# One accumulator per tile: the three products of a split fp32r block as 256-column matmuls into the same PSUM columns

## The reference, cut to what matters

```python
h = rmsnorm(x, g_pre_mix[l])
proj = h @ w_in[l]
q_in, ckv, k_rope, lru_x, lru_y, gate_mla, gate_lru = jnp.split(proj, IN_SPLIT_IDX, axis=-1)
o_mla = mla_attention(q_in, ckv, k_rope, positions, g_ckv[l], w_ukv[l]) @ w_o_mla[l]
...
merged = jax.nn.sigmoid(gate_mla) * o_mla + jax.nn.sigmoid(gate_lru) * o_lru
x = x + rmsnorm(merged @ w_out[l], g_post_mix[l])
...
x = x + rmsnorm(co @ w_co[l], g_post_x[l])
h = rmsnorm(x, g_pre_ffn[l])
up = causal_dwconv(h @ w_up[l], w_fconv[l], b_fconv[l])
gate, val = jnp.split(up, 2, axis=-1)
x = x + rmsnorm((jax.nn.gelu(gate, approximate=True) * val) @ w_down[l], g_post_ffn[l])
```

## Time and profile before

| | |
|---|---|
| median of 3 runs | 1879.62 us (1879.6 to 1880.23) |
| span of the profiled execution | 1877.5 us |
| the runs' median beside that span | 2.1 us more, for what lies around it |
| PE busy | 1798.7 us, 96% of the span |
| DVE, ACT, POOL busy | 1215.4, 973.1, 334.2 us |
| mean granted TensorE clock | 0.981 of full speed |

### The profile page before, as it was taken

How to read it: one execution, slowest core, us unless ns; L and a number is a source line. 1 busy time by engine, 2 the same in 40 slices (tenths; PEclk the granted TensorE clock), 3 DMA queues, 4 the chain that set the end, 5 groups by cost and what they waited for, 6 DMA issues and landing times.

```text
span 1877.5 us, 29213 instructions
## 1 busy us (share of the span) xinstructions
PE 1798.7 (96%) x10026; PEld 1547.0 (82%) x10026; DVE 1215.4 (65%) x1508; ACT 973.1 (52%) x1265; POOL 334.2 (18%) x375
## 2 busy tenths in 40 slices
PE   6999999999999999999998779999999999999995
PEld 5788888888888888888887558888888888888884
DVE  5666665455688874447465568776457776567776
ACT  5555555453577664445345545555345554345552
POOL 0001110000244431112243360010000000000074
PEclk9999999999999999999999879999999999999997
DMA  6544445656555565666645225657645667656561
GB/s 216 185 134 135 134 157 175 206 174 195 157 190 183 179 197 189 195 192 209 198 147 168 91 68 179 200 179 185 196 157 187 194 185 199 195 171 194 162 169 45
DMA packets 344230, 322.50 MB, mean 172 GB/s; under 512 B 5792, under 2 KB 334196, under 8 KB 343412
## 3 DMA queue, kind: packets, MB, share of 16 engines
q1 hardware_dynamic: 339124, 314.51, 53.7%
q10 hardware_dynamic: 5056, 7.34, 1.1%
HBM read 319.73 MB, written 2.10 MB: 171 GB/s over the span
## 4 chain that ended last, share of the span: by engine, by line
PE 86%; DVE 6%; ACT 3%; issue 2%; POOL 2%; DMA 0%; ACTq 0%; DVEq 0%; POOLq 0%
PE ps L414 80%; ACT wsp L822 2%; DVE wsp L1176 2%; POOL scr L1724 2%; PE ps L430 1%; PE ps L571 1%; PE ps L570 1%; PE ps L619 1%; DVE hsp L1472 1%; PE ps L477 1%; DVE big_b L1466 1%; DVE big_b L1618 0%; DVE scr L1197 0%; DMA big_a<-in_x 0%; PE ps L584 0%
## 5 line engine op out<-in xcount | busy, mean ns | idle before, releaser
L414 PE MATMUL ps<-hsp,wsp 128*128 128x512 f32 (+1 forms) x6432 | 1157.2, 341 | 19.7 <-DVE wsp L1176 8.6
L414 PEld LDWEIGHTS ps<-hsp,wsp 128*128 128x128 f32 x6432 | 992.1, 189 | 175.0 <-issue 14.0
L1176 DVE TENSOR_TENSOR wsp<-raw,wsp 128x2048 fp32r<-128x2048 f32 (+2 forms) x312 | 707.7, 2287 | 232.9 <-ACT wsp L822 230.1
L822 ACT ACTIVATE wsp<-raw 128x2048 fp32r<-128x2048 f32 (+2 forms) x312 | 580.5, 1884 | 13.8 <-PE ps L414 10.2
L414 PE MATMUL ps<-asp,wsp 128*128 128x512 f32 (+1 forms) x2816 | 505.5, 341 | 9.0 <-DVE scr L1295 4.4
L414 PEld LDWEIGHTS ps<-asp,wsp 128*128 128x128 f32 x2816 | 435.8, 190 | 75.9 <-DVE scr L1295 4.7
L833 ACT ACTIVATE cr<-ps 128x256 f32<-128x256 f32 x337 | 126.7, 381 | 546.2 <-PE ps L414 525.0
L1758 POOL TENSOR_TENSOR scr<-scr 128x256 f32<-128x256 f32 x44 | 34.2, 797 | 630.0 <-DVE scr L1556 630.0
L1184 DVE TENSOR_TENSOR cr<-ps,cr 128x256 f32<-128x256 f32 x140 | 56.9, 420 | 105.3 <-ACT cr L833 104.6
L1110 ACT ACTIVATE scr<-scr,par 128x256 f32<-128x256 f32 x88 | 48.2, 595 | 63.3 <-DVE scr L1545 63.3
L1678 POOL TENSOR_TENSOR scr<-scr 128x256 f32<-128x256 f32 x16 | 28.6, 1787 | 256.7 <-ACT scr L968 256.7
(11 more groups left out here) (180 smaller groups left out, 944.8 us busy)
## 6 DMA issues: line engine op xcount, KB each, us to landing
raw<-in_w_up SPq DMA_DIRECT2D x88, 1024.0 KB, 5.2
raw<-in_w_in SPq DMA_DIRECT2D x64, 1024.0 KB, 5.3
raw<-in_w_down SPq DMA_DIRECT2D x32, 1024.0 KB, 6.1
raw<-in_w_in SPq DMA_DIRECT2D x32, 768.0 KB, 4.2
raw<-in_w_o_mla SPq DMA_DIRECT2D x16, 1024.0 KB, 6.0
raw<-in_w_o_lru SPq DMA_DIRECT2D x16, 1024.0 KB, 5.6
raw<-in_w_out SPq DMA_DIRECT2D x16, 1024.0 KB, 5.5
raw<-in_w_down SPq DMA_DIRECT2D x16, 768.0 KB, 5.1
```

What stands on the lines that cost most here:

```text
L414: mm = pe.matmul(ps[:, bank, 0:w], lhs(part, k), x[:, 0:w], start=(f and part == 0), stop=(l and n == 1))
L822: act.activation(wsp[:, p0 % SLOTS, 0, 0:n], raw[:, p0 % SLOTS, 0:n], ACT.Copy).then_inc(hi_done, 1)
L1176: dve.tensor_tensor(wsp[:, slot, 1, 0:n], raw[:, slot, 0:n], wsp[:, slot, 0, 0:n].bitcast(F32), ALU.subtract).then_inc(lo_done, 1)
```

## The change

Each k now takes three matmuls of 256 columns, all into the first 256 columns of the bank, in the order high-high, high-low, low-high. `cross`, the buffer `cr` and the semaphores `cross_done` and `gate_done` are gone; DVE copies a finished tile from PSUM (`take`), and where a second operation followed the sum it now reads PSUM itself. The sigmoid of GM on ACT reads PSUM as well. In the first round of UP the tiles are taken out by `unit`, which stands behind `rms(7)`.

```diff
+TERMS = [(0, 0), (0, 1), (1, 0)]
...
                     f, l = first and k == 0, last and k == kn - 1
-                    parts = [1, 0] if l and not f else [0, 1]
-                    for n, part in enumerate(parts):
-                        w = T if part else 2 * T
-                        mm = pe.matmul(ps[:, bank, 0:w], lhs(part, k), x[:, 0:w], start=(f and part == 0),
-                                       stop=(l and n == 1))
+                    for n, (part, low) in enumerate(TERMS):
+                        mm = pe.matmul(ps[:, bank, 0:T], lhs(part, k), x[:, low * T:(low + 1) * T],
+                                       start=(f and n == 0), stop=(l and n == 2))
...
-            def cross(ph, i, j, slot=None, bank=None, scaled=None):
...
-                act.activation(cr[:, slot, :], ps[:, bank, T:2 * T], ACT.Copy).then_inc(cross_done, 1)
...
-            def add(ph, i, j, dst, slot=None, bank=None):
...
-                dve.wait_ge(cross_done, ph.t(i, j) + 1)
-                return dve.tensor_tensor(dst, ps[:, bank, 0:T], cr[:, slot, :], ALU.add)
+            def tile_done(ph, i, j):
+
+                dve.wait_ge(gemm_step, ph.g(i, ph.done[j]))
+
+            def take(ph, i, j, dst, bank=None):
+
+                tile_done(ph, i, j)
+                return dve.tensor_copy(dst, ps[:, j % 4 if bank is None else bank, 0:T])
...
-                    def sums(v):
-                        for j in (2 * v, 2 * v + 1):
-                            add(up, i, j, cr[:, j, :]).then_inc(tile_out, 1)
-
                     def unit(v):
 
                         for e in range(2):
-                            dve.wait_ge(tile_out, up.t(i, 2 * v + e) + 1)
-                            dve.tensor_tensor(UR[2 * v + e], cr[:, 2 * v + e, :], RR, ALU.mult).then_inc(up_ready, 1)
+                            tile_done(up, i, 2 * v + e)
+                            dve.tensor_tensor(UR[2 * v + e], ps[:, 2 * v + e, 0:T], RR, ALU.mult).then_inc(tile_out, 1)
...
                     if first:
-                        for c in (2, 3, 4):
+                        for c in (2, 3, 4, 5):
                             lo(up, i, c)
-                        sums(0)
-                        lo(up, i, 5)
-                        sums(1)
                         rms(7, norm_sum, 4, 4, D)
```

More of the change, by code:

```diff
@@ L422, in token_tile @@
                     f, l = first and k == 0, last and k == kn - 1
[L423 to L430, removed]
+                    for n, (part, low) in enumerate(TERMS):
+                        x = src[:, k0 + k, low * T + m * P:low * T + m * P + P]
+                        mm = pe.matmul(ps[:, bank, 0:T], x, rhs(k, part), start=(f and n == 0), stop=(l and n == 2))
                 if note:
@@ L838, in body @@
                         hi(ph, i, c + LEAD)
-                        if c % 2:
-                            for e in range(2):
-                                cross(ph, i, c - 1 + e)
                 rounds(act, ph, body)
@@ L860, in _ @@
                 hi(PH_A, 0, c + LEAD)
-            for j in range(5):
-                cross(PH_A, 0, j, slot=(j + 3) % 4, bank=j)
             for j in range(RT):
@@ L958, in lru @@
                 hi(ph, i, 3)
-                for e in range(2):
-                    cross(ph, i, e)
                 if not isinstance(i, int) or i:
@@ L980, in lru @@
                 hi(ph, i, 5)
-                for e in range(2):
-                    cross(ph, i, 2 + e)
             rounds(act, PH_LRU, lru, first_apart=True, last_apart=True)
@@ L1000, in o_lru @@
                         merged_hi(range(4) if c == 2 else range(4, 7))
-                    if c % 2:
-                        for e in range(2):
-                            cross(PH_OL, i, c - 1 + e)
                     if c == 1:
@@ L1018, in wo @@
                                            scale=par[:, G_MEM + k:G_MEM + k + 1]).then_inc(mem_hi, 1)
-                    if c % 2:
-                        for e in range(2):
-                            cross(PH_WO, i, c - 1 + e)
             wo(0)
@@ L1041, in _ @@
                     hi(ph, 0, c + LEAD)
-                    if c % 2:
-                        for e in range(2):
-                            cross(ph, 0, c - 1 + e)
                     if (n, c) == (0, 0):
@@ L1056, in _ @@
                         square(k, big_b[:, k, :])
-                if c == 2:
-                    for e in range(2):
-                        cross(PH_CQ, 0, e)
             root(5, RS, RV)
-            for e in range(2):
-                cross(PH_CQ, 0, 2 + e)
             def x_exps(h):
@@ L1361, in om @@
                         for e in range(2):
-                            own.mark(add(PH_OM, i, c - 1 + e, cr[:, c - 1 + e, :]))
-                        for e in range(2):
-                            dve.wait_ge(dve_self, own.now() - 1 + e)
+                            tile_done(PH_OM, i, c - 1 + e)
                             g = tile_at(big_a, i * 4 + c - 1 + e)
-                            dve.tensor_tensor(g, g, cr[:, c - 1 + e, :], ALU.mult).then_inc(tile_out, 1)
+                            dve.tensor_tensor(g, g, ps[:, c - 1 + e, 0:T], ALU.mult).then_inc(tile_out, 1)
             rounds(dve, PH_OM, om)
-            own.n, own.off = n0 + 4 * PH_OM.trips, 0
             n0 = own.n
@@ L1376, in lru @@
                 for e in range(2):
-                    add(ph, i, e, XR[e]).then_inc(tile_out, 1)
+                    take(ph, i, e, XR[e]).then_inc(tile_out, 1)
                 for e in range(2):
@@ L1569, in up_round @@
                         lo(up, i, 3)
-                    if not first:
-                        sums(0)
                     unit(0)
```

120 lines of the change are left out of this document (37 added, 83 removed).

## The result

| | before | changed |
|---|---|---|
| median | 1879.61 us (1879.03 to 1880.23, 4 runs) | 1907.89 us (1907.6 to 1908.48, 4 runs) |
| span of the profiled execution | 1877.5 us | 1906.3 us |
| mean granted clock | 0.981 | 0.981 |

The ratio is 1.0158, with a 95% interval of 1.0143 to 1.0172: 28.3 us slower, where 1909 had been forecast.

What follows compares the result with a forecast made beforehand. PE, busy for 96% of the span, was taken as the bound. Stream +32, edges -5 and new wait +5 gave +32, 1911 on the median, less 1 to 2 for low clock: 1909 us; range 1875 to 1925.

Steps and rivals of the forecast that it cites:

- The stream, +32: PE's k steps: three matmuls of 256 at 0.1195 make 0.3585 against 0.3518, times 4752 steps, +32 us.
- The 1 to 2 us off for the low clock: Stretches at half clock, three slices, pay nothing of the dearer steps: 1 to 2 us off the forecast.
- a load of 0.11 under every matmul of 0.12: In PE's runs of 256s, a weight load goes under every matmul, and any slip of one delays the other.
- rival D: PE's stream: one small fixed price for each matmul; +12 us at 0.0025, 1892, or +5 at 0.001, 1885; chance 0.13.
- rival A: The forecast itself: a 256 in a run costs 0.118 to 0.121, +10 to +53 us, likeliest 1909; chance 0.60.
- Issue, nothing: PE's queue: 4752 more matmuls with their loads cost nothing, since the sequencer is ahead.
- Places where PE waits, -5: Tiles' way out of PSUM loses a copy and some second DVE operations; where PE waits, about -5 us together.
- Cross-attention's 0.5: Before cross-attention, the shorter way out of PSUM was to save 0.5 us of PE's waiting.
- CO: Sixteen copies of 0.38 between the squares on ACT go: an estimated -1 us.
- The new wait, +5.1 net: First UP: the second round waits for the scaling behind the norm, +7.1 us, less 2 for a wait that goes.
- the old wait: PE's 1.72 us at 1148.38 for a low part that DVE made late; its going was counted as -2.
- not by 127: ACT: 337 copies of 0.381 us go, so its busy time should fall by some 127 us.

## Why the prediction came out

**The stream, +32: the rise of a step times 4752.** The forecast price, 0.1195, was 0.0005 low: 0.1200 was measured, and +39 instead of +32. I had read 0.120 as the equal half of a pair and then went under it without a reason from a row.

**The 1 to 2 us off for the low clock, and nothing else off.** This missed a credit. A slower PE waits less where low parts and norms are late, and DN was dearer before than the mean: the stream alone cost 31.4, not 39. The two errors nearly cancel, and that is luck; without it 1909 would not have lain within 1.1 us of 1907.9.

**Why a 256 is dearer behind a 256.** The explanation, a load of 0.11 under every matmul of 0.12, was wrong: with half the weights it is still 0.1200. It is a fixed price for each matmul, so this is the mechanism of rival D, for which I had written that the readings "leave it no room on average" and which I held at 0.001 to 0.0025; it is 0.0133. The price of rival A came true by the mechanism of rival D. Three matmuls pay it three times, 0.3200 + 0.0400. Two would pay 0.3467, and the step would have risen by 0.0133, 63 us; before, 24 of every 32 steps in UP and the DN of the first two groups ran on the dear footing, at about 0.353, and that hid part of it. The Trainium skill (TensorE: Matmul & The Clock Gate, section Back-to-back issue gap) gives 2.5 ns on top of the columns for the gap of a single isolated matmul, and says that this leaves out the weight load; the runs show 13.3 for these products, each with a load of its own.

**Issue, nothing.** Right: 5568 matmuls in one stretch.

**Places where PE waits, -5.** Right in kind, too small. PE's waits before and in the changed kernel: ahead of OM's second piece 1.84 and 0.55 (-1.3, forecast -1.1; 0.25 of it came with the slower stream alone); behind the last UP, for the first load, 2.02 and 0.35 (-1.7, forecast -1.1); ahead of the last norm 3.08 and 2.20 (-0.9, forecast -0.8). Cross-attention's 0.5 was right as well: 0.4 to 0.5. The term that was mis-sized is CO: 1 in the forecast, 1.8 to 1.9 measured. And one was missing: the clock in the score matmuls, 1.65 us here, which has no place in the sum and falls out differently from kernel to kernel.

**The new wait, +5.1 net.** The size came out: 6.3 us in the trace where 7.1 had been forecast, and 5.0 in all (6.8 by the traces) in the run that takes it away. The 2 us taken off for the old wait were wrong as a part of it: that wait goes even where the new one doesn't exist, and belongs to the relief of DVE and ACT. That the net figure came out at 5.1 is partly luck.

**The sum.** On the medians: stream alone +31.4, new wait +5.0, so about -8 for the edges, against a total of 28.3; on the traces +32.4, +6.8 and -10.4. ACT's busy time fell by 108 us and not by 127 because busy time counts overlapping records once. The lengths of its records together fell by 128.8 us, 128.5 of them the copies.

**What stays open.** What makes the cheap and the dear footing of alternating widths, and what in a start chooses one: shown is only that both occur in the same code, that it changes at an exchange in UP and not at one in DN, that without exchanges it changes only at waits in the two traces, and what each costs. It is also open why the clock stayed up behind a wait of 3.1 us in one kernel and not in another.

## What to carry to other kernels

Count matmuls, not only columns: here each of 256 columns or more costs 13.3 ns beyond its columns, with 64 or 128 columns of weights, so cutting a wide matmul in two has a price even where every load is hidden. A price read from a mixed stream is not the price of its parts; look at the starts of single matmuls for a pattern that changes: taking out the exchange, one line in each of two functions, gained 17.5 us, where the edit under study lost 28. Before a shorter wait is called a gain, look whether the engine only came to it later. A shorter way out of PSUM pays only where PE waits for it: apply it to those phases alone.

## What the hardware showed that was not expected

- In runs of one width, 0.1200, 0.1467 and 0.2267 us for 256, 320 and 512 columns, within 0.0001 on a line of 0.4167 ns a column and 13.3 ns a matmul; a floor of 0.1116 for 192 and 128 columns of tokens against 128 of weights.
- 512 and 256 in turn cost 0.3467 or 0.3533 a step, either for hundreds of steps. With an exchange of the two behind every 24 and 8 steps the stream goes over from one to the other each time; with one behind every 16 it stays at 0.3533. Without exchanges the same kernel ran in 1857.5 to 1860.9 us or in 1872.1.
- 512 and 384 in turn cost 0.4133, 13 ns over the line; 384 and 256 in turn 0.2938, on it.
- Behind waits of 3.12 and 3.13 us the same twelve matmuls took 2.86 us at a granted clock of 1.00 in one kernel and 4.34 at 0.64 in another.
